# A two-layer hybrid trunk on one core: the low-rank mixtures of the time-mixing layer formed by ScalarE and VectorE together

## The reference

```
def _rwkv7_mixer(x, v_first, mu, w_rkv, w0, w1, w2, a0, a1, a2, g1, g2, ...):
    xx = _token_shift(x) - x                      # x of the token before, less x
    xr, xw, xk, xv, xa, xg = (x + xx * mu[i] for i in range(6))
    r = xr @ w_rkv[0]
    k = xk @ w_rkv[1]
    v = xv @ w_rkv[2]
    w_log = -jax.nn.softplus(-(w0 + jnp.tanh(xw @ w1) @ w2)) - 0.5
    a = jax.nn.sigmoid(a0 + (xa @ a1) @ a2)
    g = jax.nn.sigmoid(xg @ g1) @ g2
    ...
```

## Time and profile before

| | us |
|---|---|
| median of three runs | 1320.22 |
| lowest, highest | 1318.19, 1326.47 |
| the profiled execution | 1314.55 |
| its span, first to last instruction | 1312.7 |
| PE busy | 1278.5 (97%) |
| DVE busy | 660.6 (50%) |
| ACT busy | 513.7 (39%) |
| POOL busy | 571.8 (44%) |
| mean granted TensorE clock | 0.998 |

### The profile page before, as it was taken

The page is one execution under the profiler, slowest core; times in us unless marked ns, Lnnn a source line. Parts: engine busy times, 40 slices in busy tenths (PEclk is TensorE's granted clock), DMA queues, the critical chain, the costliest instruction groups (busy, mean ns, idle before and its releaser), DMA issues.

```text
span 1312.7 us, 22968 instructions
## 1 busy us (share of the span) xinstructions
PE 1278.5 (97%) x9160; PEld 1056.5 (80%) x9160; DVE 660.6 (50%) x919; ACT 513.7 (39%) x868; POOL 571.8 (44%) x353
## 2 busy tenths in 40 slices
PE   6999999999999999999999999999999999999997
PEld 5888898888888887477777888888898888888885
DVE  2486731112344457854478888886641111344446
ACT  4363432223222234233345566676432222322231
POOL 5354444444444443144464455644144444444440
PEclk9999999999999999999999999999999999999999
DMA  8234243332553332175343112112443333333321
GB/s 289 65 97 129 69 141 96 96 96 80 145 140 108 104 96 65 78 256 196 129 165 125 35 51 66 36 66 82 129 128 97 96 96 96 97 96 96 96 64 65
DMA packets 113579, 139.53 MB, mean 106 GB/s; under 512 B 10416, under 2 KB 86240, under 8 KB 113504
## 3 DMA queue, kind: packets, MB, share of 16 engines
q1 hardware_dynamic: 108896, 121.67, 30.9%
q10 hardware_dynamic: 4608, 16.78, 3.4%
HBM read 123.76 MB, written 14.68 MB: 105 GB/s over the span
## 4 chain that ended last, share of the span: by engine, by line
PE 82%; DVE 10%; ACT 4%; issue 2%; DMA 1%; SPq 1%; ACTq 0%; DVEq 0%
PE bank L1797 36%; PE bank L1897 10%; PE bank L1899 10%; PE bank L1898 10%; DVE a_lo L1220 2%; DVE gram L1605 2%; PE bank L1805 2%; PE bank L1807 2%; PE bank L1806 2%; PE bank L2001 1%; PE bank L2118 1%; PE bank L1918 1%; DMA raw<-in_gm_w_in 1%; PE bank L2249 1%; PE bank L2100 1%
## 5 line engine op out<-in xcount | busy, mean ns | idle before, releaser
L498 POOL TENSOR_TENSOR w_lo<-raw,w_hi 128x1024 fp32r<-128x1024 f32 x172 | 422.4, 2461 | 581.3 <-ACT w_hi L705 533.9
L705 ACT ACTIVATE w_hi<-raw 128x1024 fp32r<-128x1024 f32 x172 | 180.5, 1056 | 283.1 <-PE bank L1797 268.6
L1797 PE MATMUL bank<-w_hi,a_hi 128*128 128x512 f32 x756 | 234.9, 392 | 5.8 <-DVE a_lo L1220 5.8
L1797 PE MATMUL bank<-w_hi,a_lo 128*128 128x512 f32 x756 | 232.9, 389 | 0.0
L1797 PE MATMUL bank<-w_lo,a_hi 128*128 128x512 f32 x756 | 232.9, 389 | 0.0
L1220 DVE TENSOR_TENSOR a_lo<-big,a_hi 128x512 fp32r<-128x512 f32 x64 | 141.3, 2213 | 178.5 <-ACT a_hi L724 175.4
L1897 PE MATMUL bank<-xT_hi,w_hi 128*128 128x512 f32 (+1 forms) x576 | 217.9, 378 | 0.0
L1899 PE MATMUL bank<-xT_hi,w_lo 128*128 128x512 f32 (+1 forms) x576 | 217.3, 377 | 0.0
L1898 PE MATMUL bank<-xT_lo,w_hi 128*128 128x512 f32 (+1 forms) x576 | 217.3, 377 | 0.0
L1364 DVE TENSOR_TENSOR big<-relu 128x512 f32 (+1 forms) x64 | 45.8, 716 | 274.4 <-ACT relu L847 274.4
L1797 PEld LDWEIGHTS bank<-w_hi,a_hi 128*128 128x128 f32 x756 | 140.1, 188 | 40.5 <-issue 12.3
(11 more groups left out here) (333 smaller groups left out, 1716.9 us busy)
## 6 DMA issues: line engine op xcount, KB each, us to landing
raw<-in_ffn_w SPq DMA_DIRECT2D x128, 512.0 KB, 3.9
raw<-in_rw_w_rkv SPq DMA_DIRECT2D x24, 512.0 KB, 3.6
raw<-in_gm_w_in SPq DMA_DIRECT2D x16, 512.0 KB, 4.2
early<-proj SPq DMA_DIRECT2D x8, 1024.0 KB, 6.4
proj<-stage ACTq DMA_DIRECT2D x14, 512.0 KB, 2.9
proj<-low_stage ACTq DMA_DIRECT2D x10, 512.0 KB, 5.1
raw<-in_gm_w_out SPq DMA_DIRECT2D x8, 512.0 KB, 3.6
late<-proj SPq DMA_DIRECT2D x8, 512.0 KB, 4.0
```

The source lines that it names most:

```text
L498: nc.gpsimd.tensor_tensor(w_lo[:, j, :], raw[:, j, :], w_hi[:, j, :].bitcast(F32), ALU.subtract).then_inc(w_lo_ready, 1)
L705: nc.scalar.activation(w_hi[:, j, :], raw[:, j, :], ACT.Copy).then_inc(w_hi_ready, 1)
L1797: last = nc.tensor.matmul(bank[2 * t + h][:], a[:, j, tok], w[:, h * HALF:(h + 1) * HALF], start=start and m == 0, stop=stop and m == 2)
```

## The change

ScalarE scales x by 1 - mu into the buffer of the low-rank mixture, and VectorE adds mu times the shifted x in place. The factors 1 - mu (`kept`) are formed once, by VectorE ahead of the first MLP of layer 0. The differences `xxT` are no longer formed ahead of the low-rank mixtures, but where the other mixtures need them: slabs 0 to 2 behind the low-rank mixtures of slabs 5 to 7, slabs 3 to 7 right ahead of the key mixtures of the same slab. The rounding of the bias and of the four key weight slabs moves within ScalarE's queue: the bias behind slab 2, two weight slabs behind slabs 4 and 6, the other two behind the sigmoids. The whole diff:

```diff
--- before.py
+++ after.py
@@ -265,6 +265,8 @@
         DONE = (TT - 1) * P
         gn = sb("gn", [P, 2, D], at=place["gains"])
         mu = sb("mu", [P, 6, KT])
+        kept = sb("kept", [P, 6, KT])
+        R_MIX, W_MIX, K_MIX, V_MIX, A_MIX, G_MIX = range(6)
         mu_rows = sb("mu_rows", [6 * KT, P])
         halves = sb("halves", [P, 2])
         select = sb("select", [P, BASE])
@@ -289,6 +291,7 @@
         gains_in, ws_arrived, bs_arrived = sem("gains_in"), sem("ws_arrived"), sem("bs_arrived")
         ident_ready, ws_masked, wsT_summed, wsT_ready = sem("ident_ready"), sem("ws_masked"), sem("wsT_summed"), sem("wsT_ready")
         x_turned, xT_ready, xT_split = sem("x_turned"), sem("xT_ready"), sem("xT_split")
+        kept_ready, lora_scaled = sem("kept_ready"), sem("lora_scaled")
         mean_ready, squares_summed = sem("mean_ready"), sem("squares_summed")
         var_ready, std_ready, x_ready, v_ready = sem("var_ready"), sem("std_ready"), sem("x_ready"), sem("v_ready")
         mixed, gated = sem("mixed"), sem("gated")
@@ -863,16 +866,27 @@
             finish_norm("down0", FT, 2, 2)
 
 
-            for j in range(SLOTS):
-                round_weights(0, j, first_slab["key"])
-            act.wait_ge(bias_in, 32)
-            nc.scalar.activation(bias_parts[:], bias[:], ACT.Copy).then_inc(bias_rounded, 1)
+            act.wait_ge(kept_ready, 1)
+            for k in range(KT):
+                act.wait_ge(xT_ready, 3 * 2 * TT - (1 if k < KT // 2 else 0))
+                if k >= 2:
+                    act.wait_ge(lora_used, k - 1)
+                for m, which in enumerate((W_MIX, A_MIX, G_MIX)):
+                    nc.scalar.activation(lora_mix[:, k % 2, m, :], xT[:, k, PAD:], ACT.Copy, scale=kept[:, which, k:k + 1]
+                                         ).then_inc(lora_scaled, 1)
+                if k == 2:
+                    act.wait_ge(bias_in, 32)
+                    nc.scalar.activation(bias_parts[:], bias[:], ACT.Copy).then_inc(bias_rounded, 1)
+                if k in (4, 6):
+                    round_weights(0, k // 2 - 2, first_slab["key"])
             act.wait_ge(wa_summed, 1)
             nc.scalar.activation(low_wa_hi[W_ROWS, :], bank[4][W_ROWS, :], ACT.Tanh).then_inc(low_ready, 1)
             nc.scalar.activation(low_wa[W_ROWS, :], bank[4][W_ROWS, :], ACT.Tanh).then_inc(low_ready, 1)
             act.wait_ge(lora_summed, 1)
             nc.scalar.activation(low_g[:], bank[6][:], ACT.Sigmoid).then_inc(low_ready, 1)
             nc.scalar.activation(low_gb[:], bank[7][:], ACT.Sigmoid).then_inc(low_ready, 1)
+            for j in range(2, SLOTS):
+                round_weights(0, j, first_slab["key"])
 
             def projected(u, t):
 
@@ -1398,25 +1412,26 @@
                 else:
                     dve.wait_ge(wa_split, j)
                     nc.vector.tensor_tensor(lo[:], raw2[:], hi[:].bitcast(F32), ALU.subtract).then_inc(wa_split, 1)
+            dve.wait_ge(mu_ready, 1)
+            nc.vector.tensor_scalar(kept[:], mu[:], -1.0, 1.0, ALU.mult, ALU.add).then_inc(kept_ready, 1)
             mlp(0, KT)
             residual_norm("down0", 1, 2, False)
-
-
-            dve.wait_ge(mu_ready, 1)
-            R_MIX, W_MIX, K_MIX, V_MIX, A_MIX, G_MIX = range(6)
 
             def mix_into(dst, k, m):
                 return nc.vector.scalar_tensor_tensor(dst, xxT[:, k, :], mu[:, m, k:k + 1], xT[:, k, PAD:],
                                                       ALU.mult, ALU.add)
+            SHIFTED = slice(PAD - 1, PAD - 1 + S)
+
+            def shift_less_x(k):
+                dve.wait_ge(xT_ready, 3 * 2 * TT)
+                then(nc.vector.tensor_tensor(xxT[:, k, :], xT[:, k, SHIFTED], xT[:, k, PAD:], ALU.subtract))
             for k in range(KT):
-
-                dve.wait_ge(xT_ready, 3 * 2 * TT - (1 if k < KT // 2 else 0))
-                then(nc.vector.tensor_tensor(xxT[:, k, :], xT[:, k, PAD - 1:PAD - 1 + S], xT[:, k, PAD:],
-                                             ALU.subtract))
-                if k >= 2:
-                    dve.wait_ge(lora_used, k - 1)
                 for m, which in enumerate((W_MIX, A_MIX, G_MIX)):
-                    mix_into(lora_mix[:, k % 2, m, :], k, which).then_inc(lora_mixed, 1)
+                    dve.wait_ge(lora_scaled, 3 * k + m + 1)
+                    nc.vector.scalar_tensor_tensor(lora_mix[:, k % 2, m, :], xT[:, k, SHIFTED], mu[:, which, k:k + 1],
+                                                   lora_mix[:, k % 2, m, :], ALU.mult, ALU.add).then_inc(lora_mixed, 1)
+                if k >= KT - 3:
+                    shift_less_x(k - (KT - 3))
             nc.vector.memset(share[:].bitcast(F32), 1.0 / Q).then_inc(ones_ready, 1)
             dve.wait_ge(bias_rounded, 1)
             for m in (1, 3):
@@ -1450,6 +1465,8 @@
                 def mix_slab(k):
                     if u * KT + k >= SLOTS:
                         dve.wait_ge(a_lo_ready, m0 + k - SLOTS + 1)
+                    if u == 0 and k >= 3:
+                        shift_less_x(k)
                     mix_into(mix[:, k % SLOTS, :], k, which).then_inc(x_mixed, 1)
                 mix_slab(0)
                 mix_slab(1)
```

## The result

The changed kernel took 1326.3 us (median of 9 runs, 1322.91 to 1328.9) against 1318.19 for the kernel before (9 runs). The ratio is 1.0051 with a 95% interval of 1.003 to 1.0072, that is +6.7 us, from 4.0 to 9.5. The forecast was +4.7 and 1324.9 us; +4.7 lies inside the interval, so the times alone don't tell it from the measurement, and the traces have to. The profiled execution went from 1314.55 to 1324.13 us (span 1312.7 to 1322.3).

What follows compares the result with a forecast made beforehand. TensorE, busy 97% of the span, was taken as the bound, so time moves only where it waits. 2.7 (loop's end, opening included) plus 2.0 (slab 6) gave +4.7 on 1320.2: 1324.9 us, range 1318.0 to 1330.5.

Steps and rivals of the forecast that it cites:

- The opening: Start of the low-rank loop: ScalarE's scaling, then the in-place mixture, make TensorE start slab 1 1.25 us late.
- The loop: Low-rank slabs: TensorE keeps pacing at 2.92 us per slab, so nothing is lost or won.
- The end of the loop: VectorE's late queue behind the low-rank loop starts projections and key product 2.7 us late, the opening's 1.25 included.
- Drains and mixture 3: Key stage: mixture 3 waits for one GpSimd operation, drains begin 0.85 us late; hidden, no cost.
- rival 3: Key stage: GpSimd keeps mixture 3 out for all four operations; sum 10.3, 1330.5 us; chance 0.05.
- Slab 6: Key product: `a_lo` of slab 6 falls just behind GpSimd and is held; TensorE reaches slab 7 2.0 us late.
- rival 1: Key product: `a_lo` of slab 6 gets ahead of GpSimd, costing 0.7 instead of 2.0; 1323.6 us; chance 0.18.
- Rival 2: Low-rank loop: VectorE paces it after all, winning 5.1 against 4.7; 1319.8 us; chance 0.05.
- Rival 4: Key product: new waits drop TensorE's clock to 1.2 GHz, costing 13 us more; 1338 us; chance 0.02.

Runs made afterwards that it cites:

- bias_in_loop: Changed kernel with VectorE's bias work and first differences moved inside the low-rank loop; ratio 1.0013 against the kernel before (0.999 to 1.0036).
- only_7_early: Changed kernel with only slab 7's difference formed early, behind the gate's drains; one execution, no ratio, landmarks +3.46 us against the kernel before.
- early_diffs: Changed kernel with the differences of slabs 4 to 7 formed together behind the gate's last drain; ratio 1.0003 against the kernel before (0.9991 to 1.0015).
- only_6_early: Changed kernel with only slab 6's difference formed early, behind the gate's drains; one execution, no ratio, landmarks +4.17 us against the kernel before.
- changed_again: The changed kernel once more, unaltered; 1323.19 us against 1315.95 for the kernel before, ratio 1.0061 (1.0037 to 1.0085).
- slab0_before: Changed kernel with slab 0's low-rank mixtures formed as in the kernel before; ratio 1.0037 against the kernel before (1.0019 to 1.0056).
- filler: Changed kernel with five products that add nothing, issued by TensorE ahead of key slab 6; ratio 1.0060 against the kernel before (1.004 to 1.0081).
- filler3: Changed kernel with three products that add nothing, issued by TensorE ahead of key slab 6; ratio 1.0040 against the kernel before (1.0024 to 1.0055).

## Why the prediction was right

It was right in its verdict and range, and both mechanisms of its sum happened at their forecast sizes. It had no term for the clock, which costs 1.54 us where the fall comes. The shift was 2.0 us short (4.7 against 6.7), the absolute time only 1.4 (1324.9 against 1326.3). The closer hit is partly luck: the forecast started from the median of three runs, 1320.22, and nine runs have 1318.19, so an error of 2.0 in the start worked against the one in the shift.

- **The opening**, forecast +1.25: measured +1.26 at slab 1 (5.63 against 4.37). The scaling takes 0.708 (0.72 taken from the earlier trace rows), the first mixture starts 1.24 behind the last copy. Its two parts were each off by 0.1 and made up for each other: slab 0 starts 1.09 later (0.98 forecast) and takes 0.17 longer (0.27 forecast).
- **The loop**, nothing won or lost: pace 2.92 in both.
- **The end of the loop**, forecast +2.7: measured +2.79. VectorE's queue is the cause: with it emptied 1.72 came back, with slab 0 restored 1.32.
- **Drains and mixture 3**, hidden: mixture 3 was held for one GpSimd operation (2.75 us) and not for four, so rival 3 failed. The key product is no later than the loop's 2.8.
- **Slab 6**, forecast +2.0: measured +2.08 where the clock held (bias_in_loop). In the changed kernel `a_lo` of slab 6 was behind GpSimd by 0.2 (0.08 forecast); rival 1 needed it ahead, and where only_7_early put it there the price was 0.65.
- **Rival 2** (VectorE paces the loop): refuted by the pace.
- **Rival 4, the clock**, chance 0.02 at +13 us: the mechanism happened and the size was wrong. The step that failed is the one that put the clock at nothing in the sum. The fall costs 1.54 us and not 13, since the clock comes back after some 3.5 us of work. (The 13 was short for its own condition: from slab 6 at 585.15 to the last product of slab 7 at 604.27 the key product had 19 us to go.) Of the five profiles with a wait of 2.3 us at this place four have the fall.

The argument against rival 4 was the flaw: a start-up wait of 2.4 us with the clock at 1.00. In the kernel before it is this one:

```profile
14.65 0.70 PE L1797 MATMUL bank<-w_hi,a_hi 128*128 128x512 f32 x2 [2.38 <-DVE a_lo L1220]
```

In other executions the same wait is followed by the same fall; here early_diffs, whose first 500 us are those of the changed kernel:

```profile
15.79 0.73 PE L1816 MATMUL bank<-w_hi,a_hi 128*128 128x512 f32 x2 [2.22 <-DVE a_lo L1234]
16.34 1.04 PE L1816 MATMUL bank<-w_lo,a_hi 128*128 128x512 f32 x2
17.17 1.06 PE L1816 MATMUL bank<-w_hi,a_lo 128*128 128x512 f32 x2
...
19.73 0.64 PE L1816 MATMUL bank<-w_hi,a_lo 128*128 128x512 f32 x2
```

Four of the thirteen profiles have it there. One execution that keeps its clock is no evidence that a wait is safe. Behind the same wait the fall came in some executions and not in others: in four of five for 2.3 us at slab 6, four of thirteen for 2.2 to 2.4 at the start, one of nine for 1.5 us at the projections, and not in the one of 1.61 us at slab 6. The Trainium skill, TensorE: Matmul & The Clock Gate, Part 1, has the clock fall to 1.2 GHz for an idle array and rise to 2.4 again once the array has been kept busy. The trace of the changed kernel agrees with both, with the fall behind the wait of 2.31 us and the rise at 595.1. Rival 4 had the fall without the rise, and so half rate for all that was left of the key product.

With the clock the structure gives 2.79 + 2.08 + 0.8 x 1.54 = 6.1 us, against 6.7 (4.0 to 9.5) and 8.0 (4.9 to 11.2) measured. The 0.8 is four profiles of five, so it is itself loose. The second interval leaves the forecast's 4.7 out.

## What to carry to other kernels

An operation of 0.7 us that is moved into a queue can cost nothing (early_diffs), 0.65 (only_7_early) or 1.38 us (only_6_early), and two of them 2.08, according to what they push behind GpSimd: look at the row behind it, not at its own duration. Price a new wait of TensorE with a short stretch at half clock times its chance on top (here 1.54 us, in four of five, for 2.3 us), and fill it with work that is ready (the next token tile) where the order allows. Work that hangs behind a loop in a queue (the bias here) belongs into the loop only as far as the queue has slack there: VectorE with 3.25 us of work in two slabs of 2.92 gave back 0.33.

## What the runs showed of the hardware

- A fall of the clock halves the rate of the matmuls (0.85 against 0.45 us per pair), begins at once (changed_again, at the start) or up to 1.2 us into the work behind the wait (slab0_before), and ends with TensorE at work: after some 3.5 us at slab 6, where it costs 1.54, and after 8.5 us at 772, where it costs 3.1. The last gap ahead of that one, 1.19 us, ends 1.9 us before it; the kernel before has the same gap, 1.21, without a fall, so that the gap is the cause is not shown.
- The kernel before has such falls too. Its one profile has them in the last 20 us alone, but its runs differ in their mean clock: of its 29 runs beside the first four experiments the two with a mean clock of 0.998 took 1313.57 and 1313.94 us, the three with 0.991 1320.54 to 1321.11. Its spread is the clock's: over its 78 runs 0.001 of mean clock goes with about 0.95 us. Landmarks in the trace hold only the falls of their own stretch. Of the twelve other profiles eleven have a fall between 700 and 910 us.
- In filler and filler3 TensorE spent the wait on matmuls with eight columns of weights (ten in 4.46 us, six in 2.74), and the granted clock from 580 to 600 us was 1.00 in both.
- Four subtractions of VectorE, all operands in SBUF, issued into GpSimd's run of four operations (early_diffs), took 7.11 us, where four at the 0.68 of one alone would take 2.7. One `a_lo` issued behind the start of a GpSimd operation took 2.48 us instead of 0.68 and ended 0.55 behind that operation's end.
